# A two-block sequence model in one kernel: other orders at three borders and four places behind them, and norms with their root by Ln and Exp and their sum, root and x in PSUM

## The reference

```python
def first_block(x, p, ...):
    x = layer_norm(x, ln_in_w, ln_in_b)
    z = x @ w_in
    z_ret, z_rwkv, z_gla, z_hgrn, z_gate = split_cols(z, GROUP_COLS)
    branches = (retnet_branch(z_ret), rwkv7_branch(z_rwkv, ...),       # four mixers, each 256 wide
                gla_branch(z_gla, ...), hgrn2_branch(z_hgrn, ...))
    merged = sum(sigmoid(gate n) * (branches[n] @ w_branch[n]) for n in range(4))
    x = layer_norm(ALPHA * x + merged @ w_mix_out, ln_mix_w, ln_mix_b)
    ffn = (gelu(causal_conv3(u)) * v) @ w_ffn_down                     # u, v = x @ w_ffn_up
    ple = sigmoid(x @ w_ple_gate) * (p @ w_ple_proj)
    return layer_norm(ALPHA * x + ffn + ple, ln_ffn_w, ln_ffn_b)

def second_block(h, ...):
    z = rmsnorm(h, norm_mix_g) @ w_in
    q, k, v, pz, ga, gp = split(z)
    a = attention(q, k, v)              # 3 groups of 4 heads, windows dilated by 1, 4, 16, ALiBi bias
    p = pool_branch(pz, w_grp, scale)   # trailing means over 2, 4, 8, 16 tokens, minus the token
    merged = sigmoid(ga) * (a @ w_att_out) + sigmoid(gp) * (p @ w_pool_out)
    h = h + merged @ w_out
    m = rmsnorm(h, norm_mlp_g)
    h = h + square(relu(m @ w_mlp_in)) @ w_mlp_out
    return rmsnorm(h, norm_final_g)
```

## Time and profile before

| | us |
|---|---|
| median of 3 runs | 3600.2 (3596.2 to 3601.91) |
| profiled execution, its own time | 3600.26 |
| profiled execution, span | 3598.4 |
| TensorE busy | 3492.9 (97%) |
| VectorE / ScalarE / GpSimd busy | 1227.8 / 1166.0 / 1288.9 |

### The profile page before, as it was taken

The page is one execution under the profiler, slowest core; times in us unless marked ns, Lnnn a source line. Parts: engine busy times, 40 slices in busy tenths (PEclk is TensorE's granted clock), DMA queues, the critical chain, the costliest instruction groups (busy, mean ns, idle before and its releaser), DMA issues.

```text
span 3598.4 us, 44630 instructions
## 1 busy us (share of the span) xinstructions
PE 3492.9 (97%) x18870; PEld 2820.3 (78%) x18870; DVE 1227.8 (34%) x1514; ACT 1166.0 (32%) x1635; POOL 1288.9 (36%) x691
## 2 busy tenths in 40 slices
PE   7999998999999999999999989999999999999998
PEld 5878886777777878888888777878886888888886
DVE  6323324545335775111111365023273221111113
ACT  4333324343323463221212344233323341202133
POOL 1312123444322654322323654211122662424265
PEclk9999999999999999999999999999999999999999
DMA  4211112231235422111112333212343331111133
GB/s 118 75 54 54 56 58 92 72 100 54 86 117 185 150 82 84 52 47 47 51 49 70 94 100 116 65 57 95 103 132 106 111 94 53 48 53 47 53 95 111
DMA packets 417029, 295.48 MB, mean 82 GB/s; under 512 B 12832, under 2 KB 385440, under 8 KB 416832
## 3 DMA queue, kind: packets, MB, share of 16 engines
q1 hardware_dynamic: 386592, 246.50, 22.8%
q10 hardware_dynamic: 30240, 46.14, 3.8%
HBM read 245.25 MB, written 47.35 MB: 81 GB/s over the span
## 4 chain that ended last, share of the span: by engine, by line
PE 86%; DVE 4%; POOL 3%; ACT 3%; issue 2%; DMA 1%; SPq 0%; POOLq 0%; DVEq 0%; ACTq 0%
PE psum L1932 56%; PE psum L266 14%; PE psum L1572 5%; PE psum L1090 2%; POOL w_lo L1883 2%; PE psum L572 2%; PE psum L1619 1%; ACT w_hi L1866 1%; PE psum L1171 1%; DVE norm_sq L2159 0%; POOL m_lo L2046 0%; PE psum L1609 0%; PE psum L1940 0%; DVE gate L3206 0%; PE psum L1083 0%
## 5 line engine op out<-in xcount | busy, mean ns | idle before, releaser
L1883 POOL TENSOR_TENSOR w_lo<-w_raw,w_hi 128x1024 fp32r<-128x1024 f32 (+1 forms) x359 | 857.6, 2389 | 1902.8 <-ACT w_hi L1866 1901.3
L1866 ACT ACTIVATE w_hi<-w_raw 128x1024 fp32r<-128x1024 f32 (+1 forms) x363 | 378.4, 1043 | 1112.9 <-PE psum L1932 1099.1
L1932 PE MATMUL psum<-x_hi,w_hi 128*128 128x512 f32 x1840 | 645.3, 393 | 11.7 <-issue 5.4
L1932 PE MATMUL psum<-x_lo,w_hi 128*128 128x512 f32 x1840 | 640.2, 390 | 0.0
L1932 PE MATMUL psum<-x_hi,w_lo 128*128 128x512 f32 x1840 | 640.2, 390 | 0.0
L1932 PEld LDWEIGHTS psum<-x_hi,w_hi 128*128 128x128 f32 x1840 | 346.5, 189 | 88.0 <-issue 16.4
L1932 PEld LDWEIGHTS psum<-x_lo,w_hi 128*128 128x128 f32 x1840 | 346.9, 189 | 73.9 <-issue 2.2
L1932 PEld LDWEIGHTS psum<-x_hi,w_lo 128*128 128x128 f32 x1840 | 346.6, 188 | 72.6
L266 PE MATMUL psum<-x_hi,w_hi 128*128 128x512 f32 x832 | 363.6, 437 | 13.3 <-POOL w_lo L1883 6.3
L266 PE MATMUL psum<-x_hi,w_lo 128*128 128x512 f32 x832 | 330.5, 397 | 0.0
L266 PE MATMUL psum<-x_lo,w_hi 128*128 128x512 f32 x832 | 329.6, 396 | 0.0
(11 more groups left out here) (550 smaller groups left out, 5395.0 us busy)
## 6 DMA issues: line engine op xcount, KB each, us to landing
w_raw<-in_w_in SPq DMA_DIRECT2D x105, 512.0 KB, 4.4
w_raw<-in_w_ffn_up SPq DMA_DIRECT2D x56, 512.0 KB, 3.8
merge_raw<-gates ACTq DMA_DIRECT2D x48, 512.0 KB, 4.4
w_raw<-in_w_mlp_in SPq DMA_DIRECT2D x48, 512.0 KB, 4.0
w_raw<-in_w_mlp_out SPq DMA_DIRECT2D x40, 512.0 KB, 4.0
gates<-gate SPq DMA_DIRECT2D x32, 512.0 KB, 2.9
w_raw<-in_w_ple_gate SPq DMA_DIRECT2D x16, 512.0 KB, 4.2
w_raw<-in_w_ffn_down SPq DMA_DIRECT2D x16, 512.0 KB, 4.1
```

The costliest lines, as they stand in the source:

```text
L1866: act.activation(self.view(self.c.wh, i), self.view(self.c.wr, i), ACT.Copy).then_inc(self.sig["w_hi"], 1)
L1883: pool.tensor_tensor(self.view(self.c.wl, i), self.view(self.c.wr, i), self.view(self.c.wh, i).bitcast(F32), ALU.subtract).then_inc(self.s ...
L1932: last = pe.matmul(self.bank(t, h)[0:m, :], w[:, k, col:col + m], x(k)[:, 512 * h:512 * h + 512], start=(k == 0 and n == 0), stop=(k == nk ...
```

## The change

It is made of six parts.

**A.** The filler of the delta-rule mixer has another order: z 0, value tile 0, z 4, turn 0, z 1, z 2, z 3, value tile 1, z 5, turn 1. The other two fillers keep theirs.

**B.** At the borders of the delta-rule, retention and hgrn mixers ScalarE makes the strips' high parts (`st.hi`) ahead of `fill.first` instead of behind it (in hgrn with the copies and exponentials that stood between). In gla only a call without effect goes.

**C.** Attention's identity and first two bias blocks lie elsewhere in SBUF and are loaded in the middle group, behind the residual's store and the last x.

**D.** Every half norm takes its inverse root as Exp(-Ln/2) on ScalarE instead of Sqrt and a reciprocal on VectorE. For ln_ffn and its RMS norm the running sum, the root and x are in PSUM banks; the last add writes to SBUF, for TensorE.

**E.** VectorE's list in the second group: the attention's low parts behind window 2 instead of 1; merge 2 behind window 4, merges 3 to 7 behind window 5.

**F.** In the second half of the last norm TensorE multiplies the running sum of seven squares and then the eighth square itself; Ln's table is loaded by a small activation at the seventh square; the root is written to PSUM for VectorE, which scales six tiles, and to SBUF for GpSimd, which scales the two others, multiplied by their gain on ScalarE; the stores are in another order.

The diff, cut:

```diff
@@ mixer, ScalarE
                     if hgrn and u == 1:
+                        st.hi(act)
                         fill.first(act)
...
             if ret:
+                st.hi(act)
                 fill.first(act)
             else:
                 logs()
-            st.hi(act)
@@ Attention.sync
-        sp.dma_start(self.ident[:, :], self.k["ident"]).then_inc(sig["ident"], 16)
-        for p in range(8):
+        sp.wait_ge(self.c.second, 16 * self.c.seconds)
+        sp.sem_inc(sig["ident"], 16)
+        sp.sem_inc(sig["bias0"], 16)
+        for p in range(1, 8):
@@ HalfNorm
+    def use(self, h, t):
+        first, mean = self.st.places[t][0], self.st.places[self.tm[h]][0]
+        others = [s for s in range(4) if s != first]
+        total = others[1] if first == mean and h == 0 else first
+        self.banks[h] = [self.c.ps[:, 2 * s + h, :] for s in (total, others[0], others[1], others[2])]
+    def total(self, h):
+        return self.banks[h][0] if self.banks else self.sq[:, 0, half(h)]
+    def root(self, h):
+        return self.banks[h][1] if self.banks else self.rstd[:, :]
+    def y(self, h, k):
+        return self.banks[h][2 + k % 2]
...
-            dve.tensor_tensor(x, x, self.sq[:, k, half(h)], ALU.add).then_inc(self.s(name), 1)
-    def deviation(self, act, t, eps):
+            dve.tensor_tensor(x if k < KT - 1 else self.sq[:, 0, half(h)], x, self.sq[:, k, half(h)], ALU.add
+                              ).then_inc(self.s(name), 1)
+    def deviation(self, act, h, t, eps, name):
+        r = self.root(h)
         self.st.done(act, t)
-        self.st.out(act.activation(self.rstd[:, :], self.st.bank(t), ACT.Sqrt, bias=eps), t)
+        self.st.out(act.activation(r, self.st.bank(t), ACT.Ln, bias=eps), t)
+        self.st.taken(act, t)
+        act.activation(r, r, ACT.Exp, scale=-0.5).then_inc(self.s(name), 1)
...
     def scale(self, dve, h):
-        self.st.taken(dve, self.tv[h])
-        dve.reciprocal(self.rstd[:, :], self.rstd[:, :]).then_inc(self.s("rstd"), 1)
         dve.wait_ge(self.s("rstd"), h + 1)
@@ middle group, SP
+            sp.wait_ge(sig["spilled"], 32)
+            sp.wait_ge(ln2.s("y"), 2 * KT)
+            bias, att_ident = att_consts
+            for dst, src in ((bias[:, 0], k["att_bias"][:, 0:2]), (att_ident[:, :], k["ident"])):
+                sp.dma_start(dst, src).then_inc(core.second, 16)
+                core.seconds += 1
             st.fetch_second(sp, second)
@@ Rms
+    def tensor_last(self, pe):
+        t = self.tiles[1]
+        self.st.start(pe, t)
+        pe.wait_ge(self.s("sum"), 2 * KT)
+        pe.matmul(self.st.bank(t), self.ones, self.c.stat[:, half(1)], start=True, stop=False)
+        pe.wait_ge(self.s("sq"), 2 * KT)
+        pe.matmul(self.st.bank(t), self.ones, self.c.square[:, half(1)], start=False, stop=True).then_inc(self.sig["mm"], 1)
+    def deviation_last(self, act):
+        t, r = self.tiles[1], self.rstd[:, :]
+        self.st.done(act, t)
+        act.wait_ge(self.s("warm"), 1)
+        self.st.out(act.activation(r, self.st.bank(t), ACT.Ln, bias=self.eps), t)
+        self.st.taken(act, t)
+        act.activation(self.st.bank(t, 1), r, ACT.Exp, scale=-0.5).then_inc(self.s("rstd"), 1)
+        act.activation(r, r, ACT.Exp, scale=-0.5).then_inc(self.s("rstd_pool"), 1)
@@ Rms.store
-        for k in range(KT):
+        for k in [n, n + 1, 0, *range(n + 2, KT - 2), *range(1, n), KT - 2, KT - 1] if h else range(KT):
@@ second group, VectorE
-                if n == 1:
+                if n == 2:
                     for h in range(2):
                         am.lo(dve, h)
-                if 3 <= n < 5:
-                    for q in (2 * n - 6, 2 * n - 5):
+                if n == 3:
+                    for q in range(2):
                         merge.vector(dve, q)
-            for q in range(4, KT):
+                if n == 4:
+                    merge.vector(dve, 2)
+            for q in range(3, KT):
                 merge.vector(dve, q)
@@ filler of the delta-rule mixer
         for n in range(4):
             fill.product(col(HGRN0 + n * P), rows(z_hgrn, n))
-        value_and(fill, HGRN0 + 512, v_hgrn, [(col(HGRN0 + 768 + n * P), rows(z_hgrn, 4 + n)) for n in range(2)])
+            if n in (0, 3):
+                value(fill, HGRN0 + 512, v_hgrn, n // 3, HGRN0 + 768, rows(z_hgrn, 4 + n // 3))
```

More of the change, by code:

```diff
@@ L1489, with __init__ @@
     COUNT = 2 * KT
-    def __init__(self, core, st, sig, mem, more, qks, vs, scratch, gates, k, w, gate0):
+    def __init__(self, core, st, sig, mem, more, consts, qks, vs, scratch, gates, k, w, gate0):
         self.c, self.st, self.sig, self.qks, self.vs, self.scratch, self.gates, self.k = (
@@ L2149, in square, with squared @@
                 self.st.taken(act, self.tm[h])
-            act.activation(self.sq[:, k, half(h)], self.c.a[:, k, half(h)], ACT.Square).then_inc(self.s("sq"), 1)
+            self.squared(act, h, k, "sq")
+    def squared(self, act, h, k, name):
+        act.activation(self.sq[:, k, half(h)] if k else self.total(h), self.c.a[:, k, half(h)], ACT.Square
+                       ).then_inc(self.s(name), 1)
     def add(self, dve, h, name, squared):
-        x = self.sq[:, 0, half(h)]
+        x = self.total(h)
         for k in range(1, KT):
@@ L2187, in affine @@
             else:
-                act.activation(self.sq[:, k, half(h)], dst, ACT.Square).then_inc(self.s("sq_rms"), 1)
+                self.squared(act, h, k, "sq_rms")
     def rms_sd(self, act, h):
-        self.deviation(act, self.tr[h], self.rms[1][:, 0:1])
+        self.deviation(act, h, self.tr[h], self.rms[1][:, 0:1], "rms_rstd")
     def rms_rstd(self, dve, h):
-        self.st.taken(dve, self.tr[h])
-        dve.reciprocal(self.rstd[:, :], self.rstd[:, :]).then_inc(self.s("rms_rstd"), 1)
         dve.wait_ge(self.s("rms_rstd"), h + 1)
@@ L2737, in first_group, with middle_group @@
     return st.place(len(st.strips) - 1)
-def middle_group(nc, core, a, k, branches, gates, stores, qks, vs, residual, ahead, second, first):
+def middle_group(nc, core, a, k, branches, gates, stores, qks, vs, residual, ahead, second, first, att_consts):
     at_ = nc.alloc_sbuf_tensor_at
@@ L2815, in middle_group @@
             qkv.plan_qk(1, n)
+        for h in range(2):
+            ln2.use(h, qkv.qk_tiles[h, 0][0])
         for n in range(6):
@@ L3306, in tensor, with gain, warm, scale_last @@
         self.st.sum(pe, self.tiles[h], self.ones, [self.c.stat[:, half(h)]])
+    def tensor_last(self, pe):
[5 more added lines that the diff above has]
+        pe.matmul(self.st.bank(t), self.ones, self.c.square[:, half(1)], start=False, stop=True).then_inc(self.sig["mm"], 1)
+    def gain(self, act, k):
+        act.wait_ge(self.s("sq"), KT + k + 1)
+        act.activation(self.c.a[:, k, half(1)], self.c.a[:, k, half(1)], ACT.Copy, scale=self.g[:, k:k + 1]
+                       ).then_inc(self.s("gain"), 1)
+    def warm(self, act):
+        act.wait_ge(self.s("y"), KT)
+        act.activation(self.rstd[:, 0:1], self.eps, ACT.Ln).then_inc(self.s("warm"), 1)
+    def deviation_last(self, act):
[6 more added lines that the diff above has]
+        act.activation(r, r, ACT.Exp, scale=-0.5).then_inc(self.s("rstd_pool"), 1)
+    def scale_last(self, dve):
+        dve.wait_ge(self.s("rstd"), 2)
+        for k in range(self.POOLED, KT):
+            x = self.c.a[:, k, half(1)]
+            dve.scalar_tensor_tensor(out=x, in0=x, scalar=self.g[:, k:k + 1], in1=self.st.bank(self.tiles[1], 1),
+                                     op0=ALU.mult, op1=ALU.mult).then_inc(self.s("y"), 1)
+    def scale_pool(self, pool):
+        pool.wait_ge(self.s("gain"), self.POOLED)
+        pool.wait_ge(self.s("rstd_pool"), 1)
+        for k in range(self.POOLED):
+            x = self.c.a[:, k, half(1)]
+            pool.tensor_tensor(x, x, self.rstd[:, :], ALU.mult).then_inc(self.s("y_pool"), 1)
     def deviation(self, act, h):
@@ L3615, in _ @@
                     last.square(act, t, m, h)
-            last.deviation(act, 1)
+                    if h and m < last.POOLED:
+                        last.gain(act, m)
+                    if (h, m) == (1, 6):
+                        last.warm(act)
+            last.deviation_last(act)
         @block.vector
@@ L3663, in _ @@
                     mlp.add(dve, KT * (LAST + h) + m)
-            last.scale(dve, 1, range(KT))
+            last.scale_last(dve)
         @block.gpsimd
@@ L3696, in _ @@
                     st.lo(pool, mlp.outs[KT * (LAST + h) + m][2])
-                    last.add(pool, h)
+                    if (h, m) < (1, KT - 1):
+                        last.add(pool, h)
+            last.scale_pool(pool)
 def constants():
@@ L3792, in phases, with value @@
     v_hgrn, v_gla, v_ret = (nc.dram_tensor("v_" + n, (T, 256), F32, kind="Internal").ap() for n in ("hgrn", "gla", "ret"))
-    def value_and(fill, c0, v, others):
-        for n in range(2):
-            fill.product(col(c0 + n * P), None)
```

(12 more changed lines are left out.)

51 lines of the change are left out of this document (29 added, 22 removed).

## The result

The changed kernel takes 3558.52 us (median of 4 runs, 3557.84 to 3562.49) against 3598.66 (4 runs): ratio 0.9892, 95% interval 0.9877 to 0.9907, so 40.1 us faster. Forecast were 3566.1 and a range of 3552 to 3586. Its profiled execution took 3562.49, span 3560.7; against the span of before that is 37.7 us. The same kernel measured once more took 3561.38 (expected: 3557 to 3561), 38.2 us less than the kernel before beside it.

A forecast was written before the change was run, and what follows sets the result against it. TensorE, busy 97% of the span, was taken as the bound, its waits and lower clock as the loss. Terms 6.8 + 1.9 + 1.3 + 11.1 + 1.6 + 4.2 + 4.2 + 3.0 = 34.1 gave 3600.2 - 34.1 = 3566.1 us, range 3552 to 3586.

The forecast's parts named there:

- the forecast case: Whole kernel: the parts' gains sum to 34.1 us, giving 3566.1 us, own range 3557 to 3574; chance 0.56.
- B's wait: Gated-recurrence border: TensorE's 6.35 us wait mostly moves one strip on, to 4 to 6 us; border gains 1.7.
- the case in which all of it goes: Rival: the seven wait places close fully, with their clock losses, 50.0 us less, 3550 us; chance 0.09.
- the wait of 3.65: Attention: the softmax moves up 2.2 us, the wait becomes 1.45 and its clock drop goes; 4.2 us gained.
- the queue on GpSimd: Gated-recurrence border: the mixer's products stand ahead of the second strip's low part, so most of the stall moves there.
- The 1.7 us of VectorE's scan: Gated-recurrence border: the scan's four parts, 3.34 us, get shorter, bringing the second strip 1.7 us earlier.
- the root comes at 2073.3 instead of 2077.5: Feed-forward norm, first half: shorter adds bring the root earlier, so scales end before the convolution's steps; stretch gains 11.1 us.
- the two waits that I kept: Feed-forward, first half: 0.75 us at a convolution behind the adds and 2.95 in the down product would remain.
- the 2.7 of the working: Last norm: the root at 3586.5 instead of 3589.25, 2.75 us earlier, is what counts; 3.0 taken for the part.
- the 3.4 us behind the last issue: Kernel's end: the 3.4 us from the eighth store's issue to the end of the span were to stay.
- waits only move: Rival: each border has a next-latest operation as near, so only 18.0 us go, 3582 us; chance 0.27.
- PSUM was free: Counters the rival that first-half projections wait for the second-half norm's bank, exposing that norm: +26.6 us, 3627; chance 0.03.

The follow-up runs named there:

- Ln and Exp alone: Kernel before, with only the half norms' root by Ln and Exp on ScalarE; sum, root and x stay in SBUF: 3599.26 us, ratio 0.9997.
- the run with fills: Kernel before, with GpSimd filling the middle group's low parts with zeros instead of subtracting, and their share of the products left out: 3573.95 us, one run.
- one more line: Changed kernel, with GpSimd making the next strip's low part ahead of level 0's products in the gated recurrence's first unit: 3555.55 us against 3561.38.
- PSUM alone: Kernel before, with only sum, root and x of the feed-forward norms in PSUM, root still by Sqrt and reciprocal: 3585.78 us, ratio 0.9956.
- root and x alone: Kernel before, with only root and x of the feed-forward norms in PSUM; running sum in SBUF, Sqrt and reciprocal kept: 3590.83 us, ratio 0.9973.
- C with E and F: Kernel before, with only the attention constants, VectorE's second-group order and the last norm changed: 3588.48 us, ratio 0.9966.

## Why the prediction was right

The sum 34.1 has to be set against 37.7 in the profile and 40.1 (38.2 the second time) in the medians. By its places the forecast case is the one that came: B's wait moved, the others went in the main. By the number alone 3558.5 lies between the forecast's 3566 and the 3550 of the case in which all of it goes.

*A* and *C* were right in mechanism, and in size within the scatter (7.4 for 6.8, 4.8 for 4.2). In C the wait of 3.65 came down to 1.50 (1.45 worked out), and the first transposes came 2.2 us earlier.

*B*: the queue on GpSimd was named as what is late next, and there it was, 4.51 us where the text had 4 to 6. The gain was ascribed to the wrong step. The 1.7 us of VectorE's scan is not what brings the second strip earlier; it is the read-out in ScalarE's queue ahead of the exponential for level 1, which the text did not see. The second strip comes 4.3 us earlier in the changed kernel. The clock that falls behind the moved wait (0.61 in the window above) was not in the sum either and takes 1.6. That 2.7 came near 1.9 is luck: two terms were left out that go against each other.

*D*: here the step "the root comes at 2073.3 instead of 2077.5, so the scales end before the convolution's own steps are late" gave the root and the operands together. The total was 1.3 us short, and the split was never worked out: the runs show 12.6 for PSUM, nothing for Ln and Exp alone, 1.4 for these on top. Of the two waits that I kept, 0.75 did not come, and 2.95 came as 1.98. At the mixer norm the root was 1.4 us earlier as worked out (Exp starts at 1276.10), but 0.8 came instead of 1.3: the eight scales take 7.75 us instead of 7.13, since they moved and GpSimd's work did not. Before, only a low part fell among them (one scale of 2.91 us); now it is GpSimd's add to the running sum for the mean at their start (one scale of 1.32) and a low part (2.90).

*E* was mis-sized: 4.2 for 5.4. The wait is 0.94, near the lower end of 0.5 to 2.2, and the slow stretch went in full (four products in 1.95 us, before 3.75). Against that stands the new stall of 0.5 at a merge, which the text did not have.

*F*: 2.3 for 3.0. VectorE's first scale comes 5.21 us after its last add instead of 7.91, the 2.7 of the working. The term that failed is the end: the 3.4 us behind the last issue are 4.3 now. The text also had the stores at least 0.6 apart, which was the pace of the scales and not of SP: some now leave 0.4 apart, and the last issue ends 5.2 us after the first scale starts, before 5.75. But stores at closer spacing land in 2.7 us (median) instead of 2.1, and from the last landing to the end of the span it is 1.95 us instead of 1.55, for which no run shows the reason. From the first scale to the end it is 9.56 us now and 9.16 before: two scales fewer on VectorE brought nothing.

Of the rivals, "waits only move" holds for B and for nothing else, and PSUM was free: no product from the first half's projections to the end of the norm waited for a bank. The rule on drains in the Trainium skill (ScalarE: Activation LUTs, What ACT_TABLE_LOAD costs) would have put 1.4 us more on each switch; in the four rows of the mixer norm's root nothing stands for more than 0.02 us. The Trainium skill's rule on who interferes (SBUF — State Buffer, Who interferes with whom) says in particular that VectorE does not contend with an instruction of GpSimd that only writes; the run with fills agrees: 11 adds beside fills, none over 0.693 us.

## What to carry to other kernels

Before shortening a step on a path, look at what its neighbours stand beside: steps of 0.68 us took up to 2.9 beside another engine that reads SBUF, and moving operands to PSUM gave 12.6 us, where removing a 3.35 us reciprocal gave nothing until then, because the steps behind it slid under that engine's next read. When a queue is reordered, read the next instruction of that queue, and what else stood behind the old one: B's first version moved 6.35 us to 4.51, one more line took the rest. Measure parts of one mechanism together as well as alone: Ln and Exp gave nothing in the feed-forward alone and 1.4 us on top of PSUM. Parts in distant stretches add up: C, E and F give the same alone and with the rest.

## What the runs showed of the hardware

The same wait does not always bring the same clock. In two profiles of the same changed kernel TensorE waits for `ffn_h_lo`, 1.98 and 1.97 us, and then runs the same products. First profile (timeline row, then the window of 3.59 us behind it), and the second:

```profile
2095.40 0.70 PE L1935 MATMUL psum<-ffn_h_hi,w_hi 128*128 128x512 f32 x1 [1.98 <-POOL ffn_h_lo L2414]
...
2095.40:2098.99 3.59, 3.59 (x9) 0.52 0.64 217
```

```profile
2093.58 0.50 PE L1935 MATMUL psum<-ffn_h_hi,w_hi 128*128 128x512 f32 x1 [1.97 <-POOL ffn_h_lo L2414]
...
2093.58:2097.17 3.59, 3.59 (x16) 1.00 0.80 277
```

In the first the granted clock is 0.52 over the stretch and 9 matmuls fit, in the second 1.00 and 16. The spans of these two profiles differ by 3.5 us: 1.6 between the feed-forward and attention, 2.2 in the three later mixers. Kernels whose code is the same in the three later mixers take from their first to their last pair product 4.3 us less to 2.5 us more than the kernel before, while their waits over 0.3 us sum to 23.1 to 26.6 us there (25.2 before); the places of the slow stretches differ. The opening shows it too: three profiles (PSUM alone, root and x alone, C with E and F) take 3.4 to 3.9 us longer up to the first product of the delta-rule mixer, with the same code and, behind the opening one, the same waits within 0.03 us (5.2, 3.4, 2.4, 1.4 and 1.0), and a clock of 0.83 between 20 and 40 us, where it is 0.91 before. Behind the opening, waits of over 3 us were followed by the lower clock in every profile; those between 1.4 and 2.5 in some. That is enough for much of the spread of 2 to 9 us between the times of one kernel here, though no run shows that it is all of it, and it is the reason why the parts were read from their stretches. What decides it in a given run stays open.
